# Attention scores as three fp32r products of high and low parts, with both rotations at other times

## The reference, cut to what matters

```
ql = _apply_rope(ql, cos, sin)           # 8 query heads of 128, latent tokens
kl = _apply_rope(kl, cos, sin)           # 2 key groups of 128
s_win = einsum('bnqkgd,bnskd->bnkgqs', qb, kw) * scale     # keys of the window (latent)
s_ctx = einsum('bnqkgd,bskd->bnkgqs', qb, kc) * scale      # keys of the context, not rotated
p = softmax(concatenate([s_win, s_ctx, s_sink], -1))       # with one sink logit per head
o = einsum(p, values)
```

## Time and profile before

| | |
|---|---|
| median of three runs | 1881.7 us |
| the profiled execution, its own time | 1880.48 us |
| its span | 1878.7 us |
| TensorE busy (matmul) | 1848.0 us, 98% of the span |
| VectorE, ScalarE, GpSimd busy | 69%, 44%, 15% |
| granted TensorE clock, mean | 0.997 of full |

### The profile page before, as it was taken

The page is one execution under the profiler, slowest core; times in us unless marked ns, Lnnn a source line. Parts: engine busy times, 40 slices in busy tenths (PEclk is TensorE's granted clock), DMA queues, the critical chain, the costliest instruction groups (busy, mean ns, idle before and its releaser), DMA issues.

```text
span 1878.7 us, 24740 instructions
## 1 busy us (share of the span) xinstructions
PE 1848.0 (98%) x10052; PEld 1563.2 (83%) x10052; DVE 1292.0 (69%) x1509; ACT 829.6 (44%) x1018; POOL 283.7 (15%) x165
## 2 busy tenths in 40 slices
PE   6999999999999999999999999999999999999998
PEld 3678888899999877887888888888888888888886
DVE  3357777776969676577767666776686568547887
ACT  3232244465555554444444445543444344434442
POOL 0000000006666262000101000220012001100100
PEclk8999999999999999999999999999999999999999
DMA  9987755544434454476776754565665566656652
GB/s 398 419 322 267 275 204 198 176 169 142 148 111 154 162 180 163 172 255 215 256 286 226 270 204 176 224 237 196 260 231 217 190 214 226 222 191 233 231 186 99
DMA packets 60321, 408.94 MB, mean 218 GB/s; under 512 B 6448, under 2 KB 9264, under 8 KB 12080
## 3 DMA queue, kind: packets, MB, share of 16 engines
q1 hardware_dynamic: 55728, 395.60, 57.7%
q10 hardware_dynamic: 4480, 11.76, 1.7%
HBM read 405.24 MB, written 2.10 MB: 217 GB/s over the span
## 4 chain that ended last, share of the span: by engine, by line
PE 89%; DMA 4%; DVE 3%; DVEq 2%; POOL 1%; ACT 1%; issue 0%; SPq 0%; ACTq 0%
PE main L1534 14%; PE main L1532 14%; PE main L1533 14%; PE side L1507 6%; PE main L1507 6%; PE main L1447 5%; PE main L1449 5%; PE main L1448 5%; DMA raw<-in_w_ad 4%; PE main L1511 3%; PE side L1511 3%; DVE wlo L976 1%; DVEq L1113 1%; PE main L1588 1%; PE main L1590 1%; PE main L1589 1%
## 5 line engine op out<-in xcount | busy, mean ns | idle before, releaser
L976 DVE TENSOR_TENSOR wlo<-raw,whi 128x1024 fp32r<-128x1024 f32 x542 | 701.7, 1322 | 298.2 <-ACT whi L493 297.6
L493 ACT CAST whi<-raw 128x1024 fp32r<-128x1024 f32 x542 | 563.3, 1050 | 700.0 <-PE main L1534 390.0
L1447 PE MATMUL main<-hCL,whi 128*128 128x256 f32 (+1 forms) x768 | 247.8, 323 | 1.0 <-DVE wlo L976 1.0
L1449 PE MATMUL main<-hCL,wlo 128*128 128x256 f32 (+1 forms) x768 | 244.5, 318 | 0.0
L1448 PE MATMUL main<-hCL,whi 128*128 128x256 f32 (+1 forms) x768 | 244.5, 318 | 0.0
L997 DVE SCALAR_TENSOR_TENSOR asum<-raw,sm,asum 128x512 f32<-128x512 f32 x240 | 211.4, 881 | 20.6 <-issue 1.8
L1534 PE MATMUL main<-whi,hid 128*128 128x512 f32 x496 | 193.1, 389 | 0.0
L1533 PE MATMUL main<-wlo,hid 128*128 128x512 f32 x496 | 193.1, 389 | 0.0
L1532 PE MATMUL main<-whi,hid 128*128 128x512 f32 x496 | 193.0, 389 | 0.0
L1507 PE MATMUL side<-h,whi 128*128 128x512 f32 x512 | 160.8, 395 | 0.0
L1532 PE MATMUL main<-whi,hCL 128*128 128x512 f32 x384 | 156.2, 407 | 0.6 <-DVE wlo L976 0.6
(11 more groups left out here) (285 smaller groups left out, 2912.6 us busy)
## 6 DMA issues: line engine op xcount, KB each, us to landing
raw<-in_w_f SPq DMA_DIRECT2D x128, 1024.0 KB, 4.8
raw<-in_w_in SPq DMA_DIRECT2D x104, 1024.0 KB, 4.9
raw<-in_w_ada SPq DMA_DIRECT2D x64, 1024.0 KB, 5.0
raw<-in_w_ad SPq DMA_DIRECT2D x32, 1024.0 KB, 14.8
raw<-in_w_br SPq DMA_DIRECT2D x24, 1024.0 KB, 5.0
raw<-in_w_out SPq DMA_DIRECT2D x16, 1024.0 KB, 4.9
xin<-in_xT SPq DMA_DIRECT2D x8, 512.0 KB, 18.0
raw<-in_w_ck SPq DMA_DIRECT2D x4, 512.0 KB, 13.3
```

The costliest lines, as they stand in the source:

```text
L493: nc.scalar.copy(half_at(q)[0], slots[slot][:, 2 * h:2 * h + 2]).then_inc(hi_made, 1)
L976: TT(half_at(q)[1], slots[slot][:, 2 * h:2 * h + 2], half_at(q)[0].bitcast(F32), ALU.subtract).then_inc(lo_made, 1)
L1447: mm(out, w_hi, x_hi, start=start, stop=False)
L1449: return mm(out, w_lo, x_hi, start=False, stop=stop)
```

## The change

The scores become three fp32r products. For that ScalarE casts the rotated queries and the group's keys to high parts (`q_hi`, `k_hi`), and GpSimd subtracts them (`q_lo` in the place of `qr`, `k_lo` in the place of `ak`). `q_hi` has the place of `qs`. The first group's attention starts one chunk later (3 instead of 2). GpSimd's first rotation waits for `y_done` 2, its second for `at_norm` 8. The second swap is moved from k = 8 to k = 22 behind `at_sc` 8. ScalarE's casts for group 0 stand at k = 2 of j = 0, for group 1 behind `pools_out`.

```
-ATTEND = 2
+ATTEND = (3, 2)
...
+        q_lo = at("q_lo", [P, 4, T], 192 * KB, F32R)
+        q_hi = at("q_hi", [P, 4, T], 162 * KB, F32R)
+        k_hi = at("k_hi", [P, C + T], 166 * KB, F32R)
+        k_lo = at("k_lo", [P, 2, C + T], 184 * KB, F32R)
...
+            def scores_high(h):                                   # ScalarE
+                act.wait_ge(at_rot, h + 1)
+                nc.scalar.copy(q_hi[:], qr[:])
+                nc.scalar.copy(k_hi[:], ak[:, h]).then_inc(qk_hi, 1)
...
-                    if j == 0 and k == 8:
-                        act.wait_ge(at_rot, 1)
+                    if j == 0 and k == 2:
+                        scores_high(0)
+                    if j == 0 and k == 22:
+                        act.wait_ge(at_sc, 8)
                         swap(1)
...
                 if j == 0:
                     pools_out()
+                    scores_high(1)
...
+            def scores_low(h):                                    # GpSimd
+                pool.wait_ge(qk_hi, h + 1)
+                TT(q_lo[:], qr[:], q_hi[:].bitcast(F32), ALU.subtract)
+                TT(k_lo[:, h], ak[:, h], k_hi[:].bitcast(F32), ALU.subtract).then_inc(qk_lo, 1)
...
+            pool.wait_ge(y_done, 2)
             rotate(0)
+            scores_low(0)
             pool.wait_ge(o_ps, 2)
             group_values(0)
...
+            pool.wait_ge(at_norm, 8)
             rotate(1)
+            scores_low(1)
             pool.wait_ge(at_o, 4)
             group_values(1)
...
                     if u == 0:                                    # TensorE, attend
-                        pe.wait_ge(at_rot, h + 1)
+                        pe.wait_ge(qk_lo, h + 1)
...
-                    mm(side[:, u % 2], qr[:, u // 2, P * (u % 2):P * (u % 2 + 1)], ak[:, h],
-                       start=True, stop=True).then_inc(at_sc, 1)
+                    own = slice(P * (u % 2), P * (u % 2 + 1))
+                    mm(side[:, u % 2], q_hi[:, u // 2, own], k_hi[:], start=True, stop=False)
+                    mm(side[:, u % 2], q_hi[:, u // 2, own], k_lo[:, h], start=False, stop=False)
+                    mm(side[:, u % 2], q_lo[:, u // 2, own], k_hi[:], start=False, stop=True).then_inc(at_sc, 1)
```

More of the change, by code:

```diff
@@ L412, in build @@
          at_v, at_sc, at_max, at_exp, at_norm, at_tr, at_cp, at_o, at_y, y_hi, y_lo, pool_diff, pool_ps, pool_y, m_done,
-         m_tr, m_hi, m_lo, ax_in, var_in, rs_out, nm_out, h2_tr, h2_hi, h2_lo, x1_done, hid_in, hid_pos, hid_hi, hid_lo, y_out, cleared, sum_hi, sum_lo, centred, diag_made, scaled, row_out) = (
+         m_tr, m_hi, m_lo, ax_in, var_in, rs_out, nm_out, h2_tr, h2_hi, h2_lo, x1_done, hid_in, hid_pos, hid_hi, hid_lo, y_out, cleared, sum_hi, sum_lo, centred, diag_made, scaled, row_out, qk_hi, qk_lo) = (
             sem(x) for x in (
@@ L418, in build @@
             "at_v at_sc at_max at_exp at_norm at_tr at_cp at_o at_y y_hi y_lo pool_diff pool_ps pool_y m_done "
-            "m_tr m_hi m_lo ax_in var_in rs_out nm_out h2_tr h2_hi h2_lo x1_done hid_in hid_pos hid_hi hid_lo y_out cleared sum_hi sum_lo centred diag_made scaled row_out").split())
+            "m_tr m_hi m_lo ax_in var_in rs_out nm_out h2_tr h2_hi h2_lo x1_done hid_in hid_pos hid_hi hid_lo y_out cleared sum_hi sum_lo centred diag_made scaled row_out qk_hi qk_lo").split())
         n_done = [sem("n_done_first"), sem("n_done_second")]
@@ L685, in attend @@
             def attend(h, k):
-                u, odd = divmod(k - ATTEND - 2, 2)
+                u, odd = divmod(k - ATTEND[h] - 2, 2)
                 if not odd and 0 <= u < 8:
@@ L693, in attend @@
                     A(c[:, 4:5], vv[:, sink:sink + 1], ACT.Exp, bias=c[:, 2:3]).then_inc(at_exp, 1)
-                u, odd = divmod(k - ATTEND - 4, 2)
+                u, odd = divmod(k - ATTEND[h] - 4, 2)
                 if not odd and 0 <= u < 8:
@@ L698, in attend @@
                                    side[:, 2].rearrange("p (a b) -> p a b", a=4)).then_inc(at_cp, 1)
-                e, rest = divmod(k - ATTEND - 8, 4)
+                e, rest = divmod(k - ATTEND[h] - 8, 4)
                 if not rest and 0 <= e < 4:
@@ L1195, in attend @@
             def attend(h, k):
-                u, odd = divmod(k - ATTEND - 3, 2)
+                u, odd = divmod(k - ATTEND[h] - 3, 2)
                 if not odd and 0 <= u < 8:
@@ L1206, in attend @@
                     TS(pr[:, u % 2], pr[:, u % 2], c[:, 6:7], None, ALU.mult).then_inc(at_norm, 1)
-                u, odd = divmod(k - ATTEND - 1, 2)
+                u, odd = divmod(k - ATTEND[h] - 1, 2)
                 if not odd and 0 <= u < 8:
@@ L1801, in attend @@
             def attend(h, k):
-                u, odd = divmod(k - ATTEND, 2)
+                u, odd = divmod(k - ATTEND[h], 2)
                 if not odd and 0 <= u < 8:
                     if u == 0:
-                        pe.wait_ge(at_rot, h + 1)
+                        pe.wait_ge(qk_lo, h + 1)
                         if h == 0:
@@ L1825, in attend @@
                     last.then_inc(at_tr, 1)
-                e, rest = divmod(k - ATTEND - 7, 4)
+                e, rest = divmod(k - ATTEND[h] - 7, 4)
                 if not rest and 0 <= e < 4:
```

## The result

The changed kernel takes 1887.14 us (median of 6 runs, 1886.98 to 1889.38) against 1881.58 us (6 runs, 1880.38 to 1882.58): ratio 1.0034, 95% interval 1.0024 to 1.0045. It is slower by 0.34% by that ratio (the two medians lie 5.6 us, 0.30%, apart). The profiled execution took 1887.26 us with a span of 1885.4; against the 1880.48 us of before that is 6.8 us more, and all of it arises in the stretch around the change: TensorE resumes after one and the same wait of the recurrence at 607.67 us here and 607.70 before, and after one and the same wait of 2.44 us in the MLP at 1164.96 here and 1158.24 before, 6.7 us later. The forecast was 1890 us, range 1879 to 1896.

What follows compares the result with a forecast made beforehand. TensorE, with matmuls busy for 98% of the span, was taken as the bound. Gains of 6.0 us and losses of 15.1 us gave net +9.1 on 1880.5, so 1890 us was forecast, range 1879 to 1896.

Steps and rivals of the forecast that it cites:

- products: TensorE's scores: sixteen fp32 products of 0.865 us become three fp32r steps, 0.68 us each; 3.0 us gained.
- waits that go: TensorE's three waits in j = 0, from both rotations and the second swap, vanish: 0.75 + 0.64 + 1.60 = 3.0 us gained.
- first group: Before its scores, the moved rotation shares turns with VectorE, making the low parts late; TensorE waits 7.1 us.
- k = 10: Transposes behind a gate block wait for reciprocal and scaling, delayed by VectorE's splits beside pooling sums; 1.5 us lost.
- second group: Start of j = 1: casts and subtractions delay the splits of chunks 1 and 2; TensorE waits, 4.3 us lost.
- slow clock: The wait before the first score product halves TensorE's clock; 2.2 us lost.
- Taking turns: In the first rotation, GpSimd and five two-input VectorE operations alternate; 7.1 us on top of 9.4 us.
- the first example's cost: Near the kernel's start, after 3.52 us idle, some 9 us of work at half speed cost 4.5 us.
- The rotation fits: Rival: no turns in the first rotation, `qk_lo` up at 642.8, before 643.95, no wait; about 1875 us, chance 0.17.

Runs made afterwards that it cites:

- experiment 9: Changed kernel with first rotation at its old time, second swap at k = 19, second group's parts early, and attention starting at four: 1875.24 us, ratio to before 0.9973.
- Experiment 10: experiment 9 with the scores as one fp32 product again, without high and low parts: 1878.59 us, ratio to before 0.999.
- experiment 5: Changed kernel with the first group's attention one chunk later still, ATTEND = (4, 2): 1886.0 us, ratio to before 1.0028.
- experiment 6: experiment 5 with ScalarE's first casts of high parts at k = 3, behind chunk 4's weight casts, instead of k = 2: 1882.28 us, ratio to before 1.0008.
- experiment 1: Changed kernel with scores as one fp32 product again, no casts or subtractions; rotations and later start stay: 1880.34 us, ratio to before 0.9999.
- experiment 4: Changed kernel with 50 unread fp32r products of 256 columns before the wait for the first scores: 1887.04 us, ratio to before 1.0034.
- experiment 8: Changed kernel with both the first rotation at its old time and the second group early (swap at k = 18): 1877.37 us, ratio to before 0.9983.
- Experiment 7: Changed kernel with second swap at k = 18, second rotation right behind it, second group's high parts ahead of pooling outputs: 1883.11 us, ratio to before 1.0016.
- experiment 2: Changed kernel with the first rotation started as before the change, GpSimd not waiting for `y_done` 2: 1880.57 us, ratio to before 0.9999.
- experiment 3: Changed kernel with the first group's attention starting at two, ATTEND = (2, 2): 1891.76 us, ratio to before 1.0059.

## Why the prediction was right

The direction, the mechanism and the place of every larger term held; the sum was too high by 2.3 us in the profiled executions. The terms, with 0.16 us added to each idle time as in the prediction:

| term | forecast | measured in the profiles |
|---|---|---|
| products | -3.0 | -3.4 (profiles of experiments 9 and 10) |
| waits that go | -3.0 | -3.0, all three gone |
| first group | +7.1 | +6.0 |
| k = 10 | +1.5 | +1.0 |
| second group | +4.3 | +3.3 (2.2 and 1.05) |
| slow clock | +2.2 | +2.7 |
| sum | +9.1 | +6.6; the profiled executions differ by 6.8 |

*Products and waits that go.* Right. Experiment 10 prices the products alone; the forecast was half a us short, since its price left out the slower steps behind an fp32 product. The 0.16 us on each wait are a little short as well: the first step behind a wait takes 0.34 us instead of 0.23 (793.37 to 793.71 in the changed kernel). This nearly cancels between the waits that go and those that come.

*First group.* "Taking turns" for five operations was right in kind: the rotation started at 628.2 as worked out and took 15.4 us instead of 9.4. The size was off in the length of a turn. I charged each operation of VectorE with its full length, 7.1 us for the five; the rotation grew by 6.0. Two splits added 2.06 us to line 920 where I had 2.4, `branch_low` 2.05 to line 921 (2.3), one split 0.99 each to lines 922 and 923 (1.2). That is the 1 us by which the rotation ended sooner than forecast, and the wait is shorter by as much. The order was off too: I let GpSimd's first operation go between the two splits of chunk 2, but both splits ran ahead of it, one behind the other. So chunk 3's first split was ready near 638.3, just in time, and the whole loss is one wait ahead of the scores; this moved 1 us from one place to another and did not change the sum. What the prediction did not have is a second layer: ScalarE's wait at k = 2 holds up the casts of chunk 4, so that a later start alone gains only 1.1 us (experiments 5 and 6). It would not have changed the sum, but it decides what mends the kernel.

*k = 10.* The wait was there for the reason given, an even k right behind a gate block beside the pooling sums. Its size is not a property of the change: 0.85 us here, 1.24 in experiment 1, 2.07 in experiments 4 and 8, where TensorE comes there at another time relative to VectorE. The bounds of 0 and 2.5 hold all of these; the 1.5 inside them was a guess, and measured were 1.0.

*Second group.* Counted from the start of j = 1 (780.75 us before, 785.51 after), chunk 1's first split was ready within 0.3 us of the forecast, and TensorE waited 2.2 us for it where I had 2.4. The second wait was mis-sized: I had VectorE's backlog shift chunk 2's splits by "about 5.5 us", where my own steps added up to 5.0 (the second split 4.4 later, the copy 0.6). They came 4.3 later (798.72 against 789.70, less the 4.76 of the start): the second split came 0.5 us sooner than forecast, and the copy held VectorE for 0.35 us, in line 1015. Experiment 7 removes both waits and gains 0.18%, 3.4 us, against the changed kernel.

*Clock.* That the wait would halve the clock was right, and 2.2 us was half of the first example's cost, a guess that came out at 2.7. That the clock term was too low while the waits were too high brought the sum nearer than its terms deserve. Experiment 4 shows that idleness is the cause. Not foreseen: waits of 2.06 and 2.07 us also brought it in some profiles and not in others.

*The rivals.* "The rotation fits" failed on its own deciding point, `k_lo` before 643.95: it came at 649.87. What it described, parts that are there in time, does exist with the rotation at another time: experiment 9 takes 1875.2 us. That it named 1875 us as well is chance, for the terms differ: experiment 9 keeps the wait at chunk 2, and its products bring half a us more.

## What to carry to other kernels

When helper work is moved away from one stall, list every operation of the engine that it shares a resource with in its new place and add them all to its length: here 9.4 us of GpSimd work became 15.4. A wait placed in the queue of an engine that also feeds the bottleneck (ScalarE before `at_rot`) holds up everything behind it, so moving only the consumer later helps little (1.1 us in experiment 5); start the producer earlier instead (6.6 us in experiment 2). And judge a repair by the trace behind it too: 2.7 us won at one place were lost to the next late operand 45 us on.

## What the runs showed of the hardware

- GpSimd's operations and VectorE's with two inputs in SBUF took turns (line 920 takes 4.45 us beside two splits, 2.39 alone; `branch_low` 4.12 beside line 920, 2.29 alone), but the turns are not strict: two VectorE splits in a row (628.05 to 630.4) went ahead of a GpSimd operation already issued at 628.21. The Trainium skill, page "SBUF — State Buffer", section "Who interferes with whom", says that issue order decides who blocks; the first split was issued earlier, the second while GpSimd was waiting. After line 920 had run, each side got one operation at a time.
- VectorE's operations with one input from PSUM were not held up: in the kernel before, lines 1216 and 1186 kept their 0.69 us each beside line 913 of the second rotation.
- The same length of wait was followed by half clock in some profiles and not in others. Of the waits of 2.06 and 2.07 us, five had it behind them: experiment 2 (0.74 in 784 to 790 us), experiment 4 at k = 10 (0.57 in 694 to 698), experiment 5 (0.76 in 790 to 793), experiment 6 (0.64 in 790 to 793) and experiment 8 (0.60 in 690 to 694). Three did not, all at the start of j = 1: the changed kernel (1.00 in 793 to 799), experiment 3 and experiment 4. What decides it was not found.
- A longer wait need not cost more slow steps: behind the 5.85 us of the changed kernel 13 steps were slow, behind the 11.2 us of experiment 3 seven. The clock had fallen at 648.8 us in the one and near 642.7 in the other, and was back near 655.2 and 653.
- How far the clock explains the spread of a kernel's runs was not shown. Experiment 7 has no wait of that length in j = 0 and j = 1 besides the one for the scores and spreads by 5.3 us, experiment 6 has one and spreads by 1.5.
